# Gates of the last prompt tile made one pass early and kept in DRAM, with other waits counted in the placing of steps

## The reference, cut to what matters

```python
h = _rms(x, ln1_g)
cq, ckv, kpe, bq, bk, bv, iq, iw, ik, ga, gb = jnp.split(h @ w_in, offs, axis=-1)
...
merged = jax.nn.sigmoid(ga) * (o_a @ w_o_a) + jax.nn.sigmoid(gb) * (o_b @ w_o_b)
x = x + merged @ w_out
t = _rms(x, ln2_g)
a = jax.nn.gelu(jnp.einsum('td,thkd->thk', t, u[e]))
x = x + jnp.einsum('thk,thkd->td', g * a, v[e])
```

## Time and profile before

| | |
|---|---|
| median of three runs | 1798.29 us |
| the profiled execution, its time | 1796.99 us |
| its span, first to last instruction | 1795.2 us |
| PE matmul busy | 1223.4 us (68%) |
| DVE busy | 1310.8 us (73%) |
| ACT busy | 579.7 us (32%) |
| POOL busy | 526.2 us (29%) |
| moved by DMA | 696.48 MB, of them 570.53 MB by the gathers' queue |
| granted TensorE clock, mean | 0.787 |

### The profile page before, as it was taken

The page is one execution under the profiler, slowest core; times in us unless marked ns, Lnnn a source line. Parts: engine busy times, 40 slices in busy tenths (PEclk is TensorE's granted clock), DMA queues, the critical chain, the costliest instruction groups (busy, mean ns, idle before and its releaser), DMA issues.

```text
span 1795.2 us, 26399 instructions
## 1 busy us (share of the span) xinstructions
PE 1223.4 (68%) x9056; PEld 679.3 (38%) x9056; DVE 1310.8 (73%) x3857; ACT 579.7 (32%) x1995; POOL 526.2 (29%) x569
## 2 busy tenths in 40 slices
PE   8989976677867575878877666679867343434343
PEld 3668532344535232444535223356535111111111
DVE  5662696989666676989666768998766878686754
ACT  2331134333423333334323334344423222222222
POOL 0200232333322223332322223232323333333332
PEclk9989889787988696897998697887999555555555
DMA  6238699999999999999999999999999999999997
GB/s 267 74 100 294 250 422 421 422 425 425 424 424 423 417 401 383 420 425 424 425 423 422 423 407 390 426 400 398 422 424 423 427 426 426 425 427 423 427 421 294
DMA packets 119381, 696.48 MB, mean 388 GB/s; under 512 B 17983, under 2 KB 21118, under 8 KB 49102
## 3 DMA queue, kind: packets, MB, share of 16 engines
q0 software_dynamic: 78848, 570.53, 76.0%
q1 hardware_dynamic: 36686, 121.83, 17.5%
q10 hardware_dynamic: 3712, 2.43, 0.4%
HBM read 691.65 MB, written 3.02 MB: 387 GB/s over the span
## 4 chain that ended last, share of the span: by engine, by line
DMA 35%; DVE 25%; PE 25%; issue 6%; ACT 3%; POOL 1%; ACTq 0%; DVEq 0%; SPq 0%; POOLq 0%
DMA rows<-in_peer_uv,index 26%; DVE rows L2657 11%; PE ps_v L1820 5%; DMA wch<-in_w_row 4%; PE ps_f L1559 4%; PE ps_f L1353 2%; PE ps_f L1574 2%; PE ps_h L1800 2%; DMA wch<-in_peer_wq 2%; DVE score L2333 1%; PE ps_f L1477 1%; PE ps_f L1653 1%; DVE best L2332 1%; DMA wch<-in_w_ukv 1%; PE ps_f L1437 1%
## 5 line engine op out<-in xcount | busy, mean ns | idle before, releaser
L2657 DVE CUSTOM_DVE_ANT_0 rows<-rows,ps_h 128x1024 f32<-128x1024 f32 x544 | 658.0, 1220 | 289.1 <-DMA rows<-in_peer_uv,index 236.3
L1330 POOL DMA_INDIRECT rows<-in_peer_uv,index x544 | 516.4, 949 | 1169.4 <-PE ps_v L1820 988.8
L1820 PE MATMUL ps_v<-rows,diag 128*32 128x256 f32 x4352 | 419.1, 500 | 432.0 <-ACT diag L2164 424.8
L1820 PEld LDWEIGHTS ps_v<-rows,diag 128*32 128x32 f32 x4352 | 124.2, 130 | 677.5 <-ACT diag L2164 561.7
L2155 ACT ACTIVATE tan<-arg 128x2 f32<-128x2 f32 x272 | 55.3, 203 | 799.2 <-DVE arg L2667 756.4
L2158 ACT ACTIVATE weight<-tan,lead 128x1 f32<-128x1 f32 x544 | 180.8, 379 | 9.1
L2164 ACT ACTIVATE diag<-sel,weight 128x32 f32<-128x32 f32 x544 | 140.9, 306 | 0.6 <-PE ps_v L1820 0.6
L1559 PEld LDWEIGHTS ps_f<-bufh,wch 128*128 128x128 f32 x768 | 103.7, 214 | 19.9 <-issue 17.8
L1559 PE MATMUL ps_f<-bufh,wch 128*128 128x128 f32 x768 | 109.7, 302 | 0.0
L1353 PE MATMUL ps_f<-wch,bufh 128*128 128x512 f32 (+1 forms) x192 | 81.9, 565 | 27.7 <-DMA wch<-in_w_row 26.7
L1653 PE MATMUL ps_f<-bufh,wch 128*128 128x128 f32 x384 | 52.1, 293 | 12.5 <-DMA wch<-in_peer_wq 12.3
(11 more groups left out here) (398 smaller groups left out, 1682.4 us busy)
## 6 DMA issues: line engine op xcount, KB each, us to landing
wch<-in_w_gate SPq DMA_DIRECT2D x60, 512.0 KB
wch<-in_w_row SPq DMA_DIRECT2D x36, 512.0 KB
wch<-in_w_o SPq DMA_DIRECT2D x32, 512.0 KB
wch<-in_w_out SPq DMA_DIRECT2D x24, 512.0 KB
wch<-in_peer_wq SPq DMA_DIRECT2D x24, 512.0 KB
rows<-in_peer_uv,index POOLq DMA_INDIRECT x544
w_tok<-in_w_tok SPq DMA_DIRECT2D x4, 1640.0 KB, 12.9
wch<-in_w_uq SPq DMA_DIRECT2D x6, 384.0 KB
```

The source lines that it names most:

```text
L1330: pool.indirect_dma_start(rows[c % RING][:, :, :].rearrange("p a d -> p (a d)"), None, io.peer_uv[:, :], at).then_inc(s_uv[c % RING], 16)
L1820: ins = nc.tensor.matmul(ps_v[GROUP * a:GROUP * (a + 1), :], diag[:, c % DRING, :], rows[c % RING][:, 1, QD * a:QD * (a + 1)], start=False ...
L2657: v.tensor_tensor_reduce(out=u, in0=u, in1=ps_h[:, :], scale=1.0, scalar=0.0, op0=ALU.mult, op1=ALU.add, accum_out=dots[:, c % KEEP:c % KE ...
```

## The change

Pass 2 (BOTH) makes the gates of prompt tile 3 beside its own. It loads that tile's x a second time into `junk`, which is `oab`, normalises and turns it in the steps x -4 to 0, which were empty, and puts the columns beside those of its own tile in `hpair`. Each gate matmul of pass 2 then has 256 columns instead of 128. ACT makes a second tanh for each of the eight j, into `qh`, and stores it, 131 KB a time, to the DRAM tensor `kept`. Pass 3 loads no gate weights and has no gate steps: SP loads `kept` back whole (1.05 MB) into `sg`. Placing: SOME = 1.5 us is counted at x 5 and at `at.rows`, HANDS = 2.4 us at x 17, in every looped pass; an empty step counts 0.5 us instead of 1.5 in passes 2 and 3.

```diff
+BOTH = 2
+ASIDE = 4
...
+SOME = 1.5
...
+    pe_head.update({5: DC * small + SOME, 17: HANDS})
...
-        pe, dve = (pe_head.get(x, 0), dve_head.get(x, 1.5 if x < 2 and p > 1 else 0)) if k < 0 else (0, 0)
+        pe, dve = (pe_head.get(x, 0), dve_head.get(x, 0.5 if x < 2 and p > 1 else 0)) if k < 0 else (0, 0)
...
+        if k == at.rows:
+            pe += SOME
...
+    apart = (pl.at - 4 * D - at_h) // 4
+    m.h_pair = Plan(nc, at_h)("hpair", [P, 2 * apart])[:, :].rearrange("p (t s) -> p t s", t=2)
...
+        if p == BOTH:
+            return m.h_pair[:, 0, 0:D].rearrange("p (c k) -> p c k", c=DC)
...
+        if p == BOTH + 1:
+            return idle_sg.rearrange("p (j a k) -> p a j k", j=DC, a=2)
...
+        return width_of(p) + (P if p == BOTH else 0)
...
+        return m.h_pair[:, :, P * k:P * (k + 1)] if p == BOTH else h_of(p)[:, k, 0:width_of(p)]
...
+    MORE = PASSES[BOTH][0] - 1
...
+        return i - 1 + (i > MORE)
...
+        return qh[:, 2 * (j % ASIDE):2 * (j % ASIDE) + 2, :]
...
-             for j in (list(range(J_AT, V_AT + 1)) + list(range(K_AT)) if p
+             for j in (list(range(J_AT, V_AT + 1)) + list(range(Z_AT if p == BOTH + 1 else 0, K_AT)) if p
...
-        return range(0 if p else SOON, DC)
+        return range(DC if p == BOTH + 1 else 0 if p else SOON, DC)
...
+                    if p == BOTH:
+                        sp.wait_ge(s_ot, 2 * (i - 1))
+                        sp.dma_start(junk, io.x_prompt[P * (t + 1):P * (t + 2), :]).then_inc(s_more_x, 16)
...
-                    for n in range(WRING):
-                        load_gate(p, n)
+                    if p <= BOTH:
+                        for n in range(WRING):
+                            load_gate(p, n)
...
+                if p == BOTH + 1:
+                    sp.wait_ge(s_pair, 3 * p)
+                    sp.wait_ge(s_qk, p)
+                    sp.wait_ge(s_new, 16 * 5 * p)
+                    for n in range(ASIDE):
+                        sp.wait_ge(s_kept[n], 16 * (DC // ASIDE))
+                    sp.dma_start(idle_sg, m.kept[:, :, :, :].rearrange("p j a k -> p (j a k)")).then_inc(s_back, 16)
+                else:
+                    for n in range(WRING + (0 if p else 2 * SOON), 2 * DC):
+                        load_gate(p, n)
...
+                if n > 1:
+                    pe.wait_ge(s_ht, 2 * (n - 1))
...
+                sums = gated(p)[:, a, :]
+                if p == BOTH:
+                    sums = sums.rearrange("p (t k) -> p t k", t=2)
                 for k in range(DC):
-                    ins = nc.tensor.matmul(gated(p)[:, a, :], w[:, k, :], h_of(p)[:, k, 0:n],
-                                           start=(k == 0), stop=(k == DC - 1))
+                    ins = nc.tensor.matmul(sums, w[:, k, :], gate_rows(p, k), start=(k == 0), stop=(k == DC - 1))
...
-                if j == 1:
+                if j == 1 and p <= BOTH:
...
+                        if x == -1 and p == BOTH:
+                            turn_x(i, MORE)
                         if x == 5:
-                            turn_x(i)
+                            turn_x(i, turn_of(i))
...
+                if p == BOTH:
+                    nc.scalar.activation(sg_of(p)[:, :, j, :], gated(p)[:, :, 0:P], ACT.Tanh, scale=0.5)
+                    if j >= ASIDE:
+                        act.wait_ge(s_kept[j % ASIDE], 16 * (j // ASIDE))
+                    nc.scalar.activation(kept_at(j), gated(p)[:, :, P:2 * P], ACT.Tanh, scale=0.5).then_inc(s_sig, 1)
+                    act.wait_ge(s_sig, gates_through(p, j))
+                    act.dma_start(m.kept[:, j, :, :], kept_at(j)).then_inc(s_kept[j % ASIDE], 16)
+                    return
...
+                if n == 0 and p == BOTH:
+                    for slot in range(ASIDE):
+                        act.wait_ge(s_kept[slot], 16 * (DC // ASIDE))
...
+                        if x == -3 and p == BOTH:
+                            root_x(MORE)
                         if x == 3:
-                            root_x(i)
+                            root_x(turn_of(i))
...
+            def more_sum():
+                dve.wait_ge(s_more_x, 16)
+                x_squares(junk)
+
+            def x_squares(x):
+                step(v.tensor_tensor_reduce(out=sq[:, 0:D], in0=x, in1=x, scale=1.0, scalar=0.0, op0=ALU.mult, op1=ALU.add,
...
+            def x_scale(p, x, n):
+                dve.wait_ge(s_rtx, n)
...
+                step(v.tensor_scalar(xin, x, px[:, 3:4], None, ALU.mult), s_xsn)
+
+            def more_columns(i):
+                dve.wait_ge(s_h, first_block(i - 1))
+                columns_out(m.h_pair[:, 1, 0:D].rearrange("p (c k) -> p c k", c=DC), MORE)
...
-                if p or j >= SOON:
+                if p == BOTH + 1:
+                    dve.wait_ge(s_back, 16)
+                elif p or j >= SOON:
...
+                        if x == -4 and p == BOTH:
+                            more_sum()
+                        if x == -2 and p == BOTH:
+                            x_scale(p, junk, MORE)
+                        if x == 0 and p == BOTH:
+                            more_columns(i)
                         if x == 2:
                             x_sum(i)
                         if x == 4:
-                            x_scale(p, i)
+                            x_scale(p, xb[i % 2][:, :], turn_of(i))
...
+    m.kept = nc.dram_tensor("kept", [P, DC, 2, P], F32).ap()
```

42 lines of the change are left out of this document (23 added, 19 removed).

## The result

The changed kernel takes 1818.59 us, the median of four runs (1815.67 to 1825.41), beside 1797.59 for the kernel before, timed next to it: the ratio is 1.0122, with a 95% interval of 1.0103 to 1.0142, so 21.9 us slower. Measured again (e12), it was 1.0138 (1.0111 to 1.0165). The forecast of 1801 and its range to 1809 were both too low. The profiled execution took 1819.41 us, its span is 1817.6 where 1795.2 stood.

A forecast was written before the change was run, and what follows sets the result against it. Time was taken as bytes over 423 GB/s plus what DMA misses, with DVE pacing pass 3's gate stretch; +1.2 + 2.5 + 6.5 + 3 - 3 - 3 - 5.6 + 1 = +2.6 us gave about 1801 us, 8-in-10 range 1788 to 1809.

The forecast's parts named there:

- pass 3 without gates: Pass 3's attention, 1110 to 1265 us: DVE's idle time above a 3.1% floor is saved, -5.6 us, bounds 0 and -10.4.
- the gates of 256 columns: Pass 2's attention: 19 us more PE work, first microseconds hidden by full DMA, +1 us, bounds 0 and +10.
- the room at `up`: Passes 2 and 3, waits for `up_out`: one column, about 3 us, more cover, booked as -3 and -3 us.
- DVE at 96% in pass 3's attention: Sign expected in the profile after: DVE at 96% or more there, waits for scores gone, rate lower than 400.
- the 8.39 MB count for nothing: Pass 3's 16 dropped gate loads lie where DVE sets the pace or just ahead, so nothing booked for them.
- rival A: Bytes decide: freed bytes are spent on gathers, 13.6 us less, 1785 us; chance 0.10.
- rival D: The counted waits open nothing: `w_uq` loads as slowly, DVE meets it a column sooner; +6, 1807 us; chance 0.08.
- The load of x, waited for early: Heads of passes 2 and 3: DVE waits some 8 us ahead of `x_sum`; +6.5 us and +3 us.
- rival B: The early wait for x is hidden by up to nine columns of gathers asked ahead: 1791 us; chance 0.20.
- rival C: PE becomes the bound in pass 2's attention, late for scores: 7 us instead of 1, 1807 us; chance 0.20.
- The extra tile in the head: Pass 2's head: square sum, root and scaling hidden in the spread wait but for the root; 2.0 us if uncovered.
- Stores, +2.5: Pass 2's attention, 720 to 900 us: 1.05 MB of stores at full DMA rate cost +2.5 us.

The follow-up runs named there:

- e12: The changed kernel itself, unaltered, timed once more beside the kernel before: 1822.3 us, ratio 1.0138.
- e10: Kernel before, old placing, pass 3's gates left out (no loads, matmuls, tanh), 1.05 MB of w_gate loaded where the kept gates would be: 1801.1 us, ratio 1.0027.
- e18: Kernel before without pass 3's gates, 1.05 MB of w_gate loaded instead of kept gates, no idle matmuls; a repeat: 1802.6 us, ratio 1.0016.
- e9: Changed kernel with pass 3's gates loaded and computed in pass 3 again, without the load back of kept gates: 1814.2 us, ratio 1.0100.
- e13: Kernel before plus pass 2's part alone (early second tile, 256-column gates, second tanh, stores); old placing, pass 3 computes its own gates: 1812.3 us, ratio 1.0078.
- e14: Kernel before plus pass 2's early second tile, second tanh and stores, but gate matmuls over 128 columns; old placing: 1805.0 us, ratio 1.0032.
- e4: Kernel before with the new counts of the placing alone, gates of one tile in each pass: 1806.5 us, ratio 1.0038.
- e5: Changed kernel with pass 2's gate matmuls over one tile's 128 columns; loads, both tanh, stores and new placing stay: 1817.0 us, ratio 1.0100.
- e15: Kernel before plus only the second tile's early load, norm and transposes; 128-column gates, no second tanh or stores, old placing: 1802.2 us, ratio 1.0022.
- e17: Kernel before without pass 3's gates, with idle matmuls of 128x128 at the gates' steps: 1795.4 us, ratio 0.9990.

## Why the prediction was wrong, step by step

The steps that failed are pass 3 without gates (-5.6 booked, +2.9 to +6.8 measured), the gates of 256 columns (+1 for 8.3), the room at `up` (-6 for 0) and what the placing does to the attention steps, for which the sum had no term. Of the signs that were named, the waits for x of about 8 us came, and so did the low rate behind column 128 (359 GB/s). DVE at 96% in pass 3's attention did not (155.2 of 182.8 us, 85%), its waits for scores were not gone (10.4 us), and pass 2's attention has a dip and waits for scores, the sign of C.

- **Pass 3 without gates, -5.6: wrong in sign.** Alone it measured +4.9 and +2.9 (e10, e18), in the changed kernel 6.8 (e12 against e9). The step took PE's relief, 31.9 us, as given and never asked what the other matmuls would take. They had run at 0.84 of the clock because of the gates. With the clock held by idle matmuls the stage was 3.7 us shorter than before and the time 1.8 less (interval -4.5 to +0.9, so not told from nothing): what gain there was, the clock ate it and more.
- **That the 8.39 MB count for nothing: right.** e9 and e10 show it from both sides, and rival A fell. DVE has 155 us to do in that stage, and bytes taken from it leave a hole in the rate.
- **Gates of 256 columns, +1: mis-sized, 8.3 measured**, inside its bounds; rival C named the mechanism and its price (7). Two errors stand in its price. The 149 ns are a difference of means of records, of which 128 matmuls make 256, so 19 us should have been 38; and the mean of overlapping matmuls is no price, the length of a batch is. They partly cancelled: PE got 25.4 us more. The step that failed is "DMA is full there, so the first microseconds hide": e13's stage from 161 to 219 is 6.3 us longer than e14's, and from there to column 256 it gives nothing back (+1.8 for +1.2). The -4.1 of the changed kernel there stands with the new placing: it is -1.9 and -2.7 in e4 and e5, whose gates are narrow.
- **More room at `up`, -3 and -3: wrong, 0.** With the one for the root, the waits at the sums of pass 2 were 7.7 us before and 8.8 after (7.6 in e12), in pass 3 11.1 and 10.1 (11.0 in e12). Why `up` came no sooner was not tried; rival D had this (+6) with a chance of 0.08.
- **The load of x, waited for early: the wait right, its price not.** 7.51 and 7.35 us of wait for "about 8". But "its gathers in flight cover nothing more" did not hold: the wait is 4.8 us longer in e4, the stage from 128 to 161 2.6, and DVE's waits for gathers between 640 and 715 us fell from 10.5 to 6.0, so rival B was right in part. As a whole the placing costs 6.8 us (e4) where these terms made 7.5 without PE's 2 and with the -6 a good 1. By e4's profile part of it lies in the attention (+2.9 and +2.9), in the waits for the spread and for `inv`, to which the prediction gave no price; that the sum without the -6 came near is luck.
- **The extra tile in the head, hidden but for the root: mis-sized.** With the old placing it costs 4.0 us together with the 0.52 MB of x (e15), as the timeline reads by the wait for the second tile's rows on PE. The 2 us for transposes were booked, the wait in front of them (4.77 us of PE in e14) not. In the changed kernel itself the head went as forecast: DVE waited 1.57 us for the root, and the dot of column 128 started at 601.28 us for 601.89. The table load took 1.28 us and the root's instruction began at its end, so the 1.38 us of drain that the prediction named beside it do not show there.
- **Stores, +2.5:** 1.8 with the second tanh, not told from nothing.

Measured alone, the parts sum to 6.8 + 14.0 + 2.9 to 4.9 = 23.7 to 25.7 us; the whole measured 21.9 and 24.8. So the parts add up to the whole within their noise.

## What to carry to other kernels

Before work is taken from TensorE, read the granted clock of the stretch: if the other matmuls there are on the path, price them at the lower level too, and test with idle matmuls in the place of the ones removed. Price a wider matmul by the length of its batch in the timeline, times the batches, and ask what is queued behind it on that engine, since at 87% busy, as here, it was late for whoever waited right behind a batch. A batch of steps moved by a few columns moves everyone's waits: time a new placing alone, on the old kernel, before it is put under another change. In a stage that one engine's busy time paces, fewer bytes show as a lower DMA rate, not as time.

## What the runs showed of the hardware that was not expected

- 128 idle matmuls of 128x128 (256 records) made a kernel 4.7 us faster (e17 beside e18): the clock of the stage went from 0.63 to 0.85, the 264-column scores from 599 to 437 ns and the mixes from 545 to 434.
- With one matmul of eight left of each half gate the stage's clock was 0.66 for 0.84 and the kernel 5.9 us slower than with all (e2).
- A matmul of fp32 shows as two records, and a batch of eight over 128 columns takes 2.05 us at the full clock, over 256 columns 3.72 (the batches at 738.11 us before and 740.37 after, granted 1.00).
